# First attention of a two-block model: keys padded with zero rows, two value heads to a matmul

## The chip, the cores and the metric

The kernel runs on one core of one Trainium2 chip, as one program. The metric is the device time of one execution in microseconds (us). Engines are called as the profile calls them: PE is TensorE (PEld its weight loads), DVE is VectorE, ACT is ScalarE, POOL is GpSimd, SP is SyncE.

## The reference, cut

The whole reference is two blocks of two layers each, from window attention through latent attention and retention to a recurrent layer. The change lies in the first layer, the window attention: 16 query heads of 64, four key and value heads (each serves four query heads), 1024 tokens in 8 tiles of 128 rows, and 256 context rows in two more tiles. A token sees the context and the keys at most 128 positions away.

```python
def window_gqa(hx, hc, w_in, sink, w_out, cos, sin, need_ctx):
    q, k, v, g = jnp.split(h @ w_in, [A_WIDTH, A_WIDTH + A_KV_WIDTH, A_WIDTH + 2 * A_KV_WIDTH], axis=-1)
    qx = apply_rope(qx, cos, sin)
    kx = apply_rope(kx, cos, sin)
    ...
        s_loc = jnp.einsum("bqhgd,bkhd->bhgqk", q, k).astype(F32) * scale
        s_loc = jnp.where(m, s_loc, -jnp.inf)
        s_ctx = jnp.einsum("bqhgd,bchd->bhgqc", q, kc).astype(F32) * scale
        p = softmax_with_sink(jnp.concatenate([s_loc, s_ctx], axis=-1), sink_b).astype(v.dtype)
        return (jnp.einsum("bhgqk,bkhd->bqhgd", p[..., :3 * BLOCK], v)
                + jnp.einsum("bhgqc,bchd->bqhgd", p[..., 3 * BLOCK:], vc))
    ...
    sc = jnp.einsum("bqhgd,bkhd->bhgqk", qc, kc).astype(F32) * scale
    pc = softmax_with_sink(sc, sink_b).astype(vc.dtype)
    oc = jnp.einsum("bhgqk,bkhd->bqhgd", pc, vc).reshape(b, hc.shape[1], A_WIDTH)
```

## The kernel before

The program is a chain of stages. Each stage is a block with one stream of instructions for each engine, tied by semaphores, and ends in a barrier of all engines. The order within a stream is the order of the Python loops; there is no scheduler. All data is float32. P is 128, BANK (a PSUM bank) 512 columns, and PSUM has eight banks.

**Projections (`window_qkv`).** For each of the ten tiles (two of context, eight of tokens) PE multiplies the normed and transposed rows by the query weights (two products of 512 columns) and by the key and value weights `w_kv` (one of 512, L585 loads them). DVE applies the rotation to queries and keys. PE turns them (`turn_heads`), and ACT copies the result from PSUM into `qT` and `kT` (L615, L617). A pair of heads stands in one 128-partition column block of `qT`: 64 partitions for each. `kT` has two such blocks, for four key heads. Pair p of query heads uses block p // 4, its lower head the lower 64 partitions and its upper head the upper ones.

**Attention (`window_attend`).** The work is cut into U = 80 units, unit u being tile u // 8 and pair u % 8. `key_tiles` gives the key tiles of a unit: two for the 16 context units, four for the 16 units of tiles 2 and 9, five for the 48 others. In a step u of PE's loop stand `scores(u)`, `transposes(u - 1)`, `sixth_bank(u)` and `values(u - 2)`:
- `scores` multiplies queries by keys for both heads of the pair, each with 64 rows (its half of the partitions), a run of neighbouring key tiles at a time (L886), into two banks for each head.
- DVE (`maxima`, L831 or L828 for the context tiles) reads the scores, adds the mask, stores them in `s_sb` and finds the row's maximum; L834 makes the bias. `scores(u + 1)` waits for both of these reads.
- ACT (`exps`, L789) takes the exponentials. PE transposes them (`transposes`, L896, four key tiles a head; the fifth in `sixth_bank`, L906), and ACT (L782) and DVE (L841) copy them to `pT`.
- `values` multiplies the value head's 64 columns by `pT`, key tile by key tile, for each head apart (L923). The lower head's result goes to PSUM partitions 0 to 63, the upper one's to 64 to 127 of one bank, `o_bank`, which holds four units.
- After four units ACT copies `o_bank` to `oT` (L804); the next `values` waits for that (L919). `sixth_bank` also turns `oT` back (L910), seven steps late, and DVE multiplies by the reciprocal of the sums (L847).

SP issues one load in this stage, of weights for the next one, into the buffer `first_weights` (called `room` in `program`).

Of the kernel before, what the change touches and what calls it, by code (L numbers as in the profile page):

```python
# [9 lines left out]
F32 = mybir.dt.float32  # L10
# [3 lines left out]
P = 128  # L14
D = 1024
KD = D // P
# [542 lines left out]

def window_qkv(nc, core, a, qT, kT, v, w_q, q_in, x_in, hT, hT_dram, mask, mask_in, sink_rows, sink_in):  # L560

# [3 lines left out]
    with ExitStack() as mem:  # L565
        sb = lambda n, shape: mem.enter_context(nc.sbuf_tensor(f"{name}_{n}", shape, F32))
        w_kv, table = sb("w_kv", [P, KD, 2 * KV]), sb("table", [P, NT, 2, A_DIM])
        xn, squares, stat = sb("xn", [P, D]), sb("squares", [P, D]), sb("stat", [P, 2])
# [5 lines left out]
             "rope_k", "q_turned", "k_turned", "qT_moved", "kT_moved"))  # L574
        hT_stored = [nc.alloc_semaphore(f"{name}_hT_stored{k}") for k in range(2)]
        cond = lambda i: 1 if i < CTX_TILES else 0
        xT_banks, q_bank, kv_bank = core.banks(0, 2), [core.banks(2), core.banks(3)], core.banks(4)
        qT_banks, kT_bank = core.banks(5, 2), core.banks(7)[:, 0:2 * P]
        HALF_STEPS, K_STEPS = 4, 4
        with nc.Block() as block:  # L580
# [17 lines left out]
            def _(act):  # L598
# [14 lines left out]
                def turned(i):  # L613
                    act.wait_ge(q_turned, i + 1)
                    act.activation(qT[:, :, i * P:(i + 1) * P], qT_banks.rearrange("p (n t) -> p n t", n=WINDOW_PAIRS), ACT.Copy).then_inc(qT_moved, 1)  # L615
                    act.wait_ge(k_turned, i + 1)
                    act.activation(kT[:, :, i * P:(i + 1) * P], kT_bank.rearrange("p (g t) -> p g t", g=2), ACT.Copy).then_inc(kT_moved, 1)  # L617

                norm(1)
                for i in range(NT):  # L620
# [5 lines left out]
                    act.activation(v[:, i, :], kv_bank[:, KV:2 * KV], ACT.Copy).then_inc(v_moved, 1)  # L626
                turned(NT - 1)

            @block.vector
# [64 lines left out]
            def _(pe):  # L694
# [8 lines left out]
                def turn_heads(i):  # L703
                    pe.wait_ge(rope_q, (i + 1) * 2 * HALF_STEPS)
                    pe.wait_ge(qT_moved, i)
                    for n in range(WINDOW_PAIRS):
                        last = pe.transpose(qT_banks[:, n * P:(n + 1) * P], qr[:, n // 4, n % 4, :, :].rearrange("p b d -> p (b d)"), core.ident)
                    last.then_inc(q_turned, 1)
                    pe.wait_ge(rope_k, (i + 1) * K_STEPS)
                    pe.wait_ge(kT_moved, i)  # L710
                    for g in range(2):
                        last = pe.transpose(kT_bank[:, g * P:(g + 1) * P], kr[:, 2 * g:2 * g + 2, :].rearrange("p b d -> p (b d)"), core.ident)
                    last.then_inc(k_turned, 1)
# [20 lines left out]
def window_attend(nc, core, a, qT, kT, v, o, mask, mask_in, sink_rows, sink_in, prefetch):  # L734
# [11 lines left out]
    with ExitStack() as mem:  # L746
# [9 lines left out]
             "pv_made", "oT_moved", "over_steps", "over_made", "back_read"))  # L756
        s_banks = [core.banks(0, 2), core.banks(2, 2)]
        pT_banks, fifth_bank, o_bank = [core.banks(4), core.banks(5)], core.banks(6), core.banks(7)
        slot = lambda u, b: pair(u) * 2 + b
# [6 lines left out]
        with nc.Block() as block:  # L766
# [6 lines left out]
            def _(act):  # L773
# [18 lines left out]
                for u in range(U + BACK):  # L792
# [5 lines left out]
                    if u >= 5 and j == 0 and w < U // 4:  # L798
                        act.wait_ge(over_steps, 3 * w + 1)
                        act.activation(halves(over, w), halves(over, w), ACT.Exp).then_inc(over_made, 1)  # L800
                        act.wait_ge(pv_made, 4 * w + 4)
                        if w >= 2:
                            act.wait_ge(fifth_made, turned_by(4 * (w - 2) + 3 + BACK))
                        act.activation(oT[:, w % 2, :, :], o_bank.rearrange("p (j q) -> p j q", j=4), ACT.Copy).then_inc(oT_moved, 1)  # L804

            @block.vector
            def _(dve):
# [9 lines left out]
                def maxima(u):  # L817
# [7 lines left out]
                    for b in range(2):  # L825
                        k = slot(u, b)
                        if t < CTX_TILES:
                            dve.tensor_scalar(s_sb[:, u % 2, b, 0:n], s_banks[b][:, 0:n], 1.0, NEG, ALU.mult, ALU.max,  # L828
                                              accum_out=smax[:, par, k:k + 1]).then_inc(s_read, 1)
                        else:  # L830
                            dve.tensor_tensor_reduce(out=s_sb[:, u % 2, b, 0:n], in0=s_banks[b][:, 0:n], in1=mask[:, lo:lo + n], scale=1.0,  # L831
                                                     scalar=NEG, op0=ALU.add, op1=ALU.max, accum_out=smax[:, par, k:k + 1]).then_inc(s_read, 1)
# [38 lines left out]
            def _(pe):  # L871
                def scores(u):
                    t, p = tile(u), pair(u)
                    if u:
                        pe.wait_ge(s_read, 2 * u)
                    runs, at = [], 0
                    for k in tiles(u):
                        if runs and runs[-1][0] + runs[-1][1] == k and at % BANK:
                            runs[-1][1] += 1
                        else:  # L880
                            runs.append([k, 1, at])
                        at += P
                    for k, n, at in runs:
                        for b in range(2):
                            rows = slice(b * A_DIM, (b + 1) * A_DIM)
                            last = pe.matmul(s_banks[b][:, at:at + n * P], qT[rows, p, t * P:(t + 1) * P], kT[rows, p // 4, k * P:(k + n) * P],  # L886
                                             start=True, stop=True)
                    last.then_inc(s_made, 1)
# [10 lines left out]
                def sixth_bank(u):  # L899
# [7 lines left out]
                    if u >= BACK:  # L907
                        n = u - BACK
                        pe.wait_ge(oT_moved, n // 4 + 1)
                        last = pe.transpose(fifth_bank[:, 2 * P:3 * P], oT[:, (n // 4) % 2, n % 4, :], core.ident)  # L910
                    last.then_inc(fifth_made, 1)

                def values(u):
# [4 lines left out]
                    if u >= 4 and u % 4 == 0:  # L918
                        pe.wait_ge(oT_moved, u // 4)  # L919
                    for n, k in enumerate(tiles(u)):  # L920
                        for b in range(2):
                            rows, g = slice(b * A_DIM, (b + 1) * A_DIM), (p // 4) * 2 + b
                            last = pe.matmul(o_bank[rows, (p % 4) * P:(p % 4 + 1) * P], v[:, k, g * A_DIM:(g + 1) * A_DIM], pT[:, u % 2, b, n, :],  # L923
                                             start=(n == 0), stop=(n == len(tiles(u)) - 1))
                    last.then_inc(pv_made, 1)
# [3434 lines left out]
def program(nc, a, out):  # L4360
    with ExitStack() as mem:
# [12 lines left out]
        with ExitStack() as layer:  # L4374
# [7 lines left out]
            with ExitStack() as keys:  # L4382
                qT = keys.enter_context(nc.sbuf_tensor("window_qT", [P, WINDOW_PAIRS, ALL_TILES * P], F32))
                kT = keys.enter_context(nc.sbuf_tensor("window_kT", [P, 2, ALL_TILES * P], F32))
                v = keys.enter_context(nc.sbuf_tensor("window_v", [P, ALL_TILES, A_KV * A_DIM], F32))
# [3 lines left out]
                with stage(nc):  # L4389
                    window_qkv(nc, core, a, qT, kT, v, o[:, 0:KD, :], q_in, x_in, hT, window_hT, mask, mask_in, sink_rows, sink_in)  # L4390
                with stage(nc):
# [116 lines left out]
```

## Time and profile before

| | us |
|---|---|
| median of 3 runs | 4081.69 |
| lowest, highest | 4074.6, 4082.69 |
| span of the profiled execution, first to last instruction | 4072.7 |
| projections stage, about | 36 to 265 of the span |
| attention stage, about | 266 to 543 of the span |

The page gives the profiled execution by its span alone. The span is the yardstick for everything read from the trace; the three runs give the times. In a timeline, a row is a run of like instructions of one engine: its start, the time from its first start to its last end, the engine, the line, the operation, the tiles and the count. A float32 matmul leaves two records on PE (a transpose leaves one), and two loads. Ends of matmuls are modelled and overlap the next one's start, so steps are read from start to start.

### The profile page before, as it was taken

Reading aid. Unit: us, or ns where it says so; the run is one execution under the profiler, and the core shown is the slowest. Engines: PE = TensorE matmul, PEld = TensorE weight load, DVE = VectorE, ACT = ScalarE, POOL = GpSimd, SP = SyncE. Lnnn points to the kernel's source line nnn. Section 1 sums busy time; section 2 is a strip of 40 time slices with the busy share of each in tenths; the row PEclk is TensorE's granted clock in tenths of the full one; section 3 lists DMA queues with packets and bytes.
Section 4 is the critical chain, followed back from the end, with each engine's and each line's share of the span. In section 5 each row is a group of like instructions: output and inputs, shape, how many; then the busy total and the mean of one; then the engine's idle time right before and its main releaser. Section 6 shows DMA issues by size and latency. Waiting matters only on the chain. (4 is left out here: it accounts for less than half of the span.)

```text
span 4072.7 us, 70205 instructions
## 1 busy us (share of the span) xinstructions
PE 3849.9 (95%) x29666; PEld 2300.5 (56%) x29666; DVE 1705.5 (42%) x3625; ACT 1216.5 (30%) x2209; POOL 803.2 (20%) x491
## 2 busy tenths in 40 slices
PE   8999999989999999999998998997999988988998
PEld 3458854445456666644554446443544468888643
DVE  3346643232144444432332008225644466565422
ACT  1147731112256556411221009112200132222124
POOL 0000023400000000142000000333112126675442
PEclk9999999999999999999999999998999999999999
DMA  6000033242321010212002000111232221212301
GB/s 227 21 21 2 2 104 114 83 103 84 118 81 39 24 48 25 74 42 73 32 16 104 16 16 28 62 42 27 83 132 85 80 86 61 70 45 88 114 6 41
DMA packets 174413, 256.15 MB, mean 63 GB/s; under 512 B 50596, under 2 KB 96148, under 8 KB 174102
## 3 DMA queue, kind: packets, MB, share of 16 engines
q1 hardware_dynamic: 174104, 251.67, 17.9%
q8 instruction: 238, 3.90, 0.4%
q14 instruction: 71, 0.58, 0.0%
HBM read 189.33 MB, written 62.05 MB: 62 GB/s over the span
## 5 line engine op out<-in xcount | busy, mean ns | idle before, releaser
L2185 DVE TENSOR_SCALAR_CACHE_REDUCE la_s<-psum 128x512 f32<-128x512 f32 (+1 forms) x384 | 210.3, 598 | 192.0 <-PE psum L2251 191.8
L2158 ACT ACTIVATE la_pT<-psum 128x512 f32<-128x512 f32 x320 | 173.0, 594 | 216.8 <-PE psum L2261 216.8
L963 POOL TENSOR_TENSOR lg_seven_s<-other_columns 128x512 f32<-128x512 f32 x4 | 5.1, 1265 | 891.4 <-POOLq L112 870.9
L2149 ACT ACTIVATE la_s<-la_s,la_negm 128x1280 f32<-128x1280 f32 x128 | 174.6, 1364 | 18.6 <-DVE la_negm L2194 14.8
L270 PE MATMUL psum<-room,columns 128*128 128x512 f32 x400 | 173.4, 592 | 0.4 <-DMA room<-in_even_w_in_dram 0.4
L2261 PE MATMUL psum<-ident,la_s 128*128 128x128 f32 x1280 | 166.2, 277 | 0.1
L2261 PEld LDWEIGHTS psum<-ident,la_s 128*128 128x128 f32 x1280 | 138.9, 140 | 40.7 <-issue 35.2
L4266 PE MATMUL psum<-rs_inverse,rs_Z 64*64 64x64 f32 x2560 | 156.3, 223 | 5.7 <-DVE rs_Z L4118 2.8
L4264 PE MATMUL psum<-rs_Z,rs_inverse 64*64 64x64 f32 x2048 | 135.6, 224 | 17.3 <-DVE rs_Z L4118 16.5
L2245 PE MATMUL psum<-la_kT,la_qT 64*128 64x512 f32 (+1 forms) x672 | 143.0, 544 | 7.4 <-DVE la_s L2185 7.4
L4266 PEld LDWEIGHTS psum<-rs_inverse,rs_Z 64*64 64x64 f32 x2560 | 136.7, 139 | 7.5 <-issue 7.3
L963 POOL TENSOR_TENSOR pg_seven_s<-pg_other_pair 128x512 f32<-128x512 f32 x4 | 6.5, 1623 | 675.6 <-ACT pg_other_pair L2863 675.6
L2272 PE MATMUL psum<-la_pT,la_v 128*64 128x128 f32 x2240 | 134.6, 275 | 0.7 <-ACT la_pT L2158 0.7
L831 DVE CUSTOM_DVE_ANT_0 wa_s<-psum,window_mask_rows 128x640 f32<-128x640 f32 (+1 forms) x128 | 100.7, 787 | 71.5 <-PE psum L886 71.5
L270 PEld LDWEIGHTS psum<-room,columns 128*128 128x128 f32 x400 | 75.9, 190 | 96.4 <-issue 96.1
L4264 PEld LDWEIGHTS psum<-rs_Z,rs_inverse 64*64 64x64 f32 x2048 | 117.9, 140 | 20.2 <-issue 18.6
L2272 PEld LDWEIGHTS psum<-la_pT,la_v 128*64 128x64 f32 x2240 | 121.2, 137 | 10.1 <-issue 9.0
L963 POOL TENSOR_TENSOR wg_seven_s<-other_columns 128x512 f32<-128x512 f32 x5 | 6.3, 1269 | 591.6 <-POOLq L112 543.8
L4126 DVE TENSOR_TENSOR rs_inverse<-rs_inverse,psum 128x512 f32<-128x512 f32 (+1 forms) x160 | 101.1, 632 | 45.2 <-PE psum L4266 44.5
L789 ACT ACTIVATE wa_s<-wa_s,wa_negm 128x640 f32<-128x640 f32 (+2 forms) x160 | 117.3, 742 | 0.4 <-DVE wa_negm L834 0.3
L4251 PE MATMUL psum<-rs_inverse,rs_A 64*64 64x64 f32 x2560 | 107.2, 222 | 10.5 <-DVE rs_inverse L4112 8.8
L984 PE MATMUL psum<-rp_t,rp_seven_s 128*128 128x512 f32 x256 | 115.7, 595 | 0.0
(674 smaller groups left out, 8198.8 us busy)
## 6 DMA issues: line engine op xcount, KB each, us to landing
later_slot<-in_ada_w_dram SPq DMA_DIRECT2D x16, 1024.0 KB
rwkv_raw<-x_rows SPq DMA_DIRECT2D x64, 256.0 KB, 2.0
room<-rwkv_raw SPq DMA_DIRECT2D x32, 512.0 KB, 4.7
room<-in_even_w_in_dram SPq DMA_DIRECT2D x6, 2048.0 KB, 9.4
room<-in_odd_w_in_dram SPq DMA_DIRECT2D x6, 2048.0 KB, 12.7
ada_slots<-in_ada_w_dram SPq DMA_DIRECT2D x8, 1024.0 KB, 9.4
rwkv_raw<-room SPq DMA_DIRECT2D x16, 512.0 KB, 2.6
latent_v<-lp_v SPq DMA_DIRECT2D x10, 512.0 KB, 2.8
```

The lines of the kernel that those rows point to most:

```text
L270: last = pe.matmul(out[:, c:c + w], left[:, k, :], right[:, k, c:c + w], start=(k == 0), stop=(k == kd - 1))
L789: act.activation(s_sb[:, u % 2, b, 0:n], s_sb[:, u % 2, b, 0:n], ACT.Exp, scale=SCALE, bias=negm[:, par, k:k + 1], accum_out=total[:, par, ...
L984: last = pe.matmul(bank, left[:, k, :], right[:, k, :], start=fresh and k == 0, stop=k == HK - 1, skip_group_check=True)
L2149: act.activation(s_sb[:, g % 2, j, :], s_sb[:, g % 2, j, :], ACT.Exp, bias=negm[:, g % 2, j:j + 1], accum_out=total[:, g % 2, j:j + 1]).th ...
L2158: act.activation(pT[:, h, at * BANK:(at + 1) * BANK], pT_banks[turn], ACT.Copy).then_inc(pT_moved[turn], 1)
L2185: dve.tensor_scalar(s_sb[:, g % 2, j, cols], s_banks[j][:, 0:cols.stop - cols.start], SCALE, NEG, ALU.mult, ALU.max, accum_out=smax[:, g % ...
L2245: pe.matmul(s_banks[unit(h, i)][:, 0:width], q_of[rows, queries(i)], k_of[rows, cols], start=True, stop=False)
L2261: last = pe.transpose(pT_banks[turn][:, n * P:(n + 1) * P], s_sb[:, g % 2, j, t * P:(t + 1) * P], core.ident)
L2272: last = pe.matmul(o_banks[h][i * B_V:(i + 1) * B_V, 0:P], v_of[:, t, h * B_V:(h + 1) * B_V], pT[:, h, i * K + t * P:i * K + (t + 1) * P], ...
L4251: last = pe.matmul(core.banks(2 + m % 2)[chunk(c), n * C:(n + 1) * C], A[chunk(c), 0, h, 0, :], T[chunk(c), h, :], start=True, stop=True)
L4264: pe.matmul(bank[chunk(c), n * C:(n + 1) * C], TT[chunk(c), h, :], Z[chunk(c), h, :], start=True, stop=True)
L4266: last = pe.matmul(bank[chunk(c), (GH + n) * C:(GH + n + 1) * C], Z[chunk(c), h, :], TT[chunk(c), h, :], start=True, stop=True)
```

## The change

Keys. `kT` gets four blocks in place of two, one for each key head: its 64 rows stand where its query head's rows stand in `qT`, and the other 64 partitions are zero. POOL writes the zeros (four memsets) during the projections. ACT copies the keys in two instructions of 64 partitions where it had one of 128. The room for the wider `kT` comes from `w_kv`, which moves to the buffer `first_weights`.

Scores. Each head's scores are one product over all 128 partitions with both heads' queries; the rows of the other head meet zeros. The scores of both heads stand one behind the other in three banks instead of two and two, cut where a bank ends.

Values. One matmul for each key tile covers both heads: stationary are two value heads' 128 columns, moving are both heads' 256 columns of `pT`. The result is 128x256, of which two of four quarters are wanted. Four units need two banks (`o_banks`), and ACT copies the wanted quarters in two instructions.

```diff
-        w_kv, table = sb("w_kv", [P, KD, 2 * KV]), sb("table", [P, NT, 2, A_DIM])
+        table = sb("table", [P, NT, 2, A_DIM])
...
-                    act.activation(kT[:, :, i * P:(i + 1) * P], kT_bank.rearrange("p (g t) -> p g t", g=2), ACT.Copy).then_inc(kT_moved, 1)
+                    for b in range(2):
+                        rows = slice(b * A_DIM, (b + 1) * A_DIM)
+                        act.activation(kT[rows, b:A_KV:2, i * P:(i + 1) * P], kT_bank[rows, :].rearrange("p (g t) -> p g t", g=2), ACT.Copy).then_inc(kT_moved, 1)
...
+            @block.gpsimd
+            def _(pool):
+                for b in range(2):
+                    other = slice((1 - b) * A_DIM, (2 - b) * A_DIM)
+                    for g in range(2):
+                        pool.memset(kT[other, 2 * g + b, :], 0.0).then_inc(padded, 1)
+                pool.wait_ge(padded, A_KV)
...
-        s_banks = [core.banks(0, 2), core.banks(2, 2)]
-        pT_banks, fifth_bank, o_bank = [core.banks(4), core.banks(5)], core.banks(6), core.banks(7)
+        s_banks, o_banks = core.banks(0, 3), core.banks(3, 2)
+        pT_banks, fifth_bank = [core.banks(5), core.banks(6)], core.banks(7)
+        scores_of = lambda u, b: s_banks[:, b * len(tiles(u)) * P:(b + 1) * len(tiles(u)) * P]
+        o_of = lambda j: o_banks[:, j * 2 * P:(j + 1) * 2 * P]
...
-                        act.activation(oT[:, w % 2, :, :], o_bank.rearrange("p (j q) -> p j q", j=4), ACT.Copy).then_inc(oT_moved, 1)
+                        for b in range(2):
+                            rows = slice(b * A_DIM, (b + 1) * A_DIM)
+                            act.activation(oT[rows, w % 2, :, :], o_banks[rows, :].rearrange("p (j b q) -> p j b q", j=4, b=2)[:, :, b, :], ACT.Copy).then_inc(oT_moved, 1)
...
-                    runs, at = [], 0
-                    for k in tiles(u):
...
-                    for k, n, at in runs:
-                        for b in range(2):
-                            rows = slice(b * A_DIM, (b + 1) * A_DIM)
-                            last = pe.matmul(s_banks[b][:, at:at + n * P], qT[rows, p, t * P:(t + 1) * P], kT[rows, p // 4, k * P:(k + n) * P],
-                                             start=True, stop=True)
+                    for b in range(2):
+                        runs, at = [], b * len(tiles(u)) * P
+                        for k in tiles(u):
...
+                        for k, n, at in runs:
+                            last = pe.matmul(s_banks[:, at:at + n * P], qT[:, p, t * P:(t + 1) * P], kT[:, 2 * (p // 4) + b, k * P:(k + n) * P], start=True, stop=True)
...
-                        for b in range(2):
-                            rows, g = slice(b * A_DIM, (b + 1) * A_DIM), (p // 4) * 2 + b
-                            last = pe.matmul(o_bank[rows, (p % 4) * P:(p % 4 + 1) * P], v[:, k, g * A_DIM:(g + 1) * A_DIM], pT[:, u % 2, b, n, :],
-                                             start=(n == 0), stop=(n == len(tiles(u)) - 1))
+                        last = pe.matmul(o_of(p % 4), v[:, k, (p // 4) * 2 * A_DIM:(p // 4 + 1) * 2 * A_DIM], pT[:, u % 2, :, n, :],
+                                         start=(n == 0), stop=(n == len(tiles(u)) - 1))
...
-                kT = keys.enter_context(nc.sbuf_tensor("window_kT", [P, 2, ALL_TILES * P], F32))
+                kT = keys.enter_context(nc.sbuf_tensor("window_kT", [P, A_KV, ALL_TILES * P], F32))
...
-                    window_qkv(nc, core, a, qT, kT, v, o[:, 0:KD, :], q_in, x_in, hT, window_hT, mask, mask_in, sink_rows, sink_in)
+                    window_qkv(nc, core, a, qT, kT, v, o[:, 0:KD, :], room, q_in, x_in, hT, window_hT, mask, mask_in, sink_rows, sink_in)
```

PE's stream in a unit of five key tiles, before (matmuls are listed once each; the last number is the shape written, partitions by columns):

```order
L886 MATMUL psum<-window_kT,window_qT 128x256 x4
L886 MATMUL psum<-window_kT,window_qT 128x128 x2
L896 MATMUL psum<-ident,wa_s 128x128 x8
L906 MATMUL psum<-ident,wa_s 128x128 x2
L910 MATMUL psum<-ident,wa_oT 128x128
L923 MATMUL psum<-wa_pT,window_v 64x128 x10
```

The same unit after:

```order
L900 MATMUL psum<-window_kT,window_qT 128x256 x2
L900 MATMUL psum<-window_kT,window_qT 128x128
L900 MATMUL psum<-window_kT,window_qT 128x256
L900 MATMUL psum<-window_kT,window_qT 128x128 x3
L909 MATMUL psum<-ident,wa_s 128x128 x8
L919 MATMUL psum<-ident,wa_s 128x128 x2
L923 MATMUL psum<-ident,wa_oT 128x128
L934 MATMUL psum<-wa_pT,window_v 128x256 x5
```

Six score matmuls become seven, ten values matmuls of 64x128 become five of 128x256; the order of the four groups and the eleven transposes stay. The second place is ACT's stream around the copy to `oT` in the units of four and five key tiles, before:

```order
L789 ACTIVATE wa_s,wa_total<-wa_s,wa_negm 128x512 x2
L800 ACTIVATE wa_over<-wa_over 128x8
L804 ACTIVATE wa_oT<-psum 128x512
L782 ACTIVATE wa_pT<-psum 128x512 x2
L789 ACTIVATE wa_s,wa_total<-wa_s,wa_negm 128x512 x2
```

and after:

```order
L802 ACTIVATE wa_s,wa_total<-wa_s,wa_negm 128x512 x2
L813 ACTIVATE wa_over<-wa_over 128x8
L819 ACTIVATE wa_oT<-psum 64x512 x2
L795 ACTIVATE wa_pT<-psum 128x512 x2
L802 ACTIVATE wa_s,wa_total<-wa_s,wa_negm 128x512 x2
```

One copy becomes two of half the partitions, at the same place.

## Rows read from the trace of the kernel before

**Rows 1.** The page's head: the span, and PE's busy time and instructions.

```profile
span 4072.7 us, 70205 instructions
...
PE 3849.9 (95%) x29666; PEld 2300.5 (56%) x29666; DVE 1705.5 (42%) x3625; ACT 1216.5 (30%) x2209; POOL 803.2 (20%) x491
```

**Rows 2.** Busy time by stretch: start:end, length, busy us (count) of each engine.

```profile
core 0: us, PE busy (x) PEld busy (x) DVE busy (x) ACT busy (x) POOL busy (x), PEclk, DMA share, GB/s
60.00:265.00 205.00, 203.37 (x596) 98.86 (x594) 73.33 (x135) 27.51 (x58) 0.00 (x0) 1.00 0.04 17
...
361.00:392.00 31.00, 31.00 (x348) 26.61 (x346) 21.10 (x71) 22.74 (x53) 0.00 (x0) 1.00 0.01 1
```

**Rows 3.** Waits of 300 to 530 us: total us, times, the longest.

```profile
DVE wa_s L831 <- PE psum L886: 69.8, 62, 1.4
ACT wa_pT L782 <- PE psum L896: 57.9, 61, 1.2
...
PE psum L886 <- DVE wa_smax L831: 0.4, 1, 0.4
```

**Rows 4.** Timeline of PE, one unit of five key tiles: start, us, line, count.

```profile
400.02 1.35 PE L886 MATMUL psum<-window_kT,window_qT 64*128 64x256 f32 x12
401.31 1.09 PE L896 MATMUL psum<-ident,wa_s 128*128 128x128 f32 x8
402.24 0.38 PE L906 MATMUL psum<-ident,wa_s 128*128 128x128 f32 x2
402.46 0.27 PE L910 MATMUL psum<-ident,wa_oT 128*128 128x128 f32 x1
402.66 1.31 PE L923 MATMUL psum<-wa_pT,window_v 128*64 128x128 f32 x20
403.90 0.49 PE L886 MATMUL psum<-window_kT,window_qT 64*128 64x256 f32 x2
```

**Rows 5.** Timeline of PE, a unit of four key tiles (tile 9).

```profile
518.92 1.14 PE L886 MATMUL psum<-window_kT,window_qT 64*128 64x256 f32 x8
519.99 1.09 PE L896 MATMUL psum<-ident,wa_s 128*128 128x128 f32 x8
...
521.12 1.09 PE L923 MATMUL psum<-wa_pT,window_v 128*64 128x128 f32 x16
522.14 1.14 PE L886 MATMUL psum<-window_kT,window_qT 64*128 64x256 f32 x8
```

**Rows 6.** Timeline of PE, a unit of two key tiles: its scores and the next unit's.

```profile
288.29 0.70 PE L886 MATMUL psum<-window_kT,window_qT 64*128 64x256 f32 x4
...
290.20 0.70 PE L886 MATMUL psum<-window_kT,window_qT 64*128 64x256 f32 x4
```

**Rows 7.** Timeline of PE, dense runs on the full array in other stages.

```profile
232.24 1.04 PE L707 MATMUL psum<-ident,wq_qr 128*128 128x128 f32 x8
...
233.33 7.03 PE L270 MATMUL psum<-wq_w_kv,columns 128*128 128x512 f32 x16
...
2535.62 1.95 PE L2744 MATMUL psum<-stick_v,sk_wT 128*128 128x128 f32 x16
```

**Rows 8.** Groups by line and shape, 264 to 545 us: busy us, mean ns, idle before.

```profile
L886 PEld LDWEIGHTS psum<-window_kT,window_qT 64*128 64x128 f32 x800 | 69.5, 187 | 22.5 <-issue 12.7 <-DVE wa_s L828 3.8 <-DVE wa_smax L831 1.0
...
L804 ACT ACTIVATE wa_oT<-psum 128x512 f32<-128x512 f32 x20 | 11.8, 590 | 1.7 <-PE psum L923 1.7
...
L963 POOL TENSOR_TENSOR wg_seven_s<-other_columns 128x512 f32<-128x512 f32 x1 | 1.3, 1264 | 543.8 <-POOLq L112 543.8
```

**Rows 9.** Timeline: the last keys of the projections, the last copy of the attention.

```profile
263.94 0.44 PE L712 MATMUL psum<-ident,wq_kr 128*128 128x128 f32 x2 [1.02 <-DVE wq_kr L679]
264.42 0.38 ACT L617 ACTIVATE window_kT<-psum 128x256 f32<-128x256 f32 x1 [0.43 <-PE psum L712]
...
539.22 0.60 ACT L804 ACTIVATE wa_oT<-psum 128x512 f32<-128x512 f32 x1 [1.73 <-PE psum L923]
```

**Rows 10.** One line of another stage, its weight loads: ns min/median/max.

```profile
L2744 PEld LDWEIGHTS psum<-stick_v,sk_wT x288: 186/192/333, 2445.1 to 2548.0; 128*128 128x128 f32 x144
```

More of the change, by code:

```diff
@@ L557, with window_qkv @@
 WINDOW_PAIRS = A_HEADS // 2
-def window_qkv(nc, core, a, qT, kT, v, w_q, q_in, x_in, hT, hT_dram, mask, mask_in, sink_rows, sink_in):
+def window_qkv(nc, core, a, qT, kT, v, w_q, w_kv, q_in, x_in, hT, hT_dram, mask, mask_in, sink_rows, sink_in):
     name = "wq"
@@ L575, in window_qkv @@
         hT_stored = [nc.alloc_semaphore(f"{name}_hT_stored{k}") for k in range(2)]
+        padded = nc.alloc_semaphore(f"{name}_padded")
         cond = lambda i: 1 if i < CTX_TILES else 0
@@ L709, in turn_heads @@
                     pe.wait_ge(rope_k, (i + 1) * K_STEPS)
-                    pe.wait_ge(kT_moved, i)
+                    pe.wait_ge(kT_moved, 2 * i)
                     for g in range(2):
@@ L827, in maxima @@
                         if t < CTX_TILES:
-                            dve.tensor_scalar(s_sb[:, u % 2, b, 0:n], s_banks[b][:, 0:n], 1.0, NEG, ALU.mult, ALU.max,
+                            dve.tensor_scalar(s_sb[:, u % 2, b, 0:n], scores_of(u, b), 1.0, NEG, ALU.mult, ALU.max,
                                               accum_out=smax[:, par, k:k + 1]).then_inc(s_read, 1)
                         else:
-                            dve.tensor_tensor_reduce(out=s_sb[:, u % 2, b, 0:n], in0=s_banks[b][:, 0:n], in1=mask[:, lo:lo + n], scale=1.0,
+                            dve.tensor_tensor_reduce(out=s_sb[:, u % 2, b, 0:n], in0=scores_of(u, b), in1=mask[:, lo:lo + n], scale=1.0,
                                                      scalar=NEG, op0=ALU.add, op1=ALU.max, accum_out=smax[:, par, k:k + 1]).then_inc(s_read, 1)
@@ L875, in scores @@
                         pe.wait_ge(s_read, 2 * u)
-                    runs, at = [], 0
-                    for k in tiles(u):
[L878 to L882, printed above, removed]
-                    for k, n, at in runs:
-                        for b in range(2):
-                            rows = slice(b * A_DIM, (b + 1) * A_DIM)
-                            last = pe.matmul(s_banks[b][:, at:at + n * P], qT[rows, p, t * P:(t + 1) * P], kT[rows, p // 4, k * P:(k + n) * P],
-                                             start=True, stop=True)
+                    for b in range(2):
+                        runs, at = [], b * len(tiles(u)) * P
+                        for k in tiles(u):
+                            if runs and runs[-1][0] + runs[-1][1] == k and at % BANK:
+                                runs[-1][1] += 1
+                            else:
+                                runs.append([k, 1, at])
+                            at += P
+                        for k, n, at in runs:
+                            last = pe.matmul(s_banks[:, at:at + n * P], qT[:, p, t * P:(t + 1) * P], kT[:, 2 * (p // 4) + b, k * P:(k + n) * P], start=True, stop=True)
                     last.then_inc(s_made, 1)
@@ L908, in sixth_bank @@
                         n = u - BACK
-                        pe.wait_ge(oT_moved, n // 4 + 1)
+                        pe.wait_ge(oT_moved, 2 * (n // 4 + 1))
                         last = pe.transpose(fifth_bank[:, 2 * P:3 * P], oT[:, (n // 4) % 2, n % 4, :], core.ident)
@@ L918, in values @@
                     if u >= 4 and u % 4 == 0:
-                        pe.wait_ge(oT_moved, u // 4)
+                        pe.wait_ge(oT_moved, 2 * (u // 4))
                     for n, k in enumerate(tiles(u)):
-                        for b in range(2):
-                            rows, g = slice(b * A_DIM, (b + 1) * A_DIM), (p // 4) * 2 + b
-                            last = pe.matmul(o_bank[rows, (p % 4) * P:(p % 4 + 1) * P], v[:, k, g * A_DIM:(g + 1) * A_DIM], pT[:, u % 2, b, n, :],
-                                             start=(n == 0), stop=(n == len(tiles(u)) - 1))
+                        last = pe.matmul(o_of(p % 4), v[:, k, (p // 4) * 2 * A_DIM:(p // 4 + 1) * 2 * A_DIM], pT[:, u % 2, :, n, :],
+                                         start=(n == 0), stop=(n == len(tiles(u)) - 1))
                     last.then_inc(pv_made, 1)
```

## The prediction

> **What bounds the kernel now.** I read the page's head first: PE is busy 95% of a span of 4072.7 us [rows 1]. The change touches two stages, so next the busy times by stretch [rows 2]: the projections (60 to 265 us) keep PE busy 203.4 of 205 us, with DVE at 73 and ACT at 28; in the attention, 361 to 392 us, PE is busy 31.00 of 31.00 us, ACT 22.7 and DVE 21.1, at a granted clock of 1.00, the upper level, 2.4 GHz. The waits of 300 to 530 us say who waits for whom [rows 3]: DVE waited 69.8 us for the scores and ACT 57.9 us for the transposes, while PE waited once, for 0.4 us. So here each ns added to PE's queue is a ns of the stage, and a ns added to ACT or DVE is free as long as it fits under PE.
>
> The stage is 80 units (ten query tiles by eight head pairs). In its steady part a unit takes 3.88 us, from 400.02 to 403.90 [rows 4]: scores 1.29, eleven transposes 1.35, values 1.24. With four key tiles a unit takes 3.22 us (518.92 to 522.14) [rows 5], with two 1.91 [rows 6]. There are 48 units of five key tiles, 16 of four, 16 of two.
>
> **How PE's time is made.** Each float32 matmul leaves two records (six score matmuls, x12). The full-array price comes from dense runs elsewhere [rows 7]. Sixteen records of 512 columns span 7.03 us; less the last one's own 0.592 that is 15 steps of 0.429. Sixteen of 128 columns span 1.95; less 0.275 it is 15 steps of 0.112. A straight line through both gives 0.218 for 256 columns. Transposes go at (1.04 - 0.273) / 7 = 0.110.
>
> Now the same sizes when two records use different halves of the array. The values matmuls of before write 64 columns each, one head in either half: 16 records of 128 columns span 1.09 us [rows 5], where the full array needs 1.95 for the same 16 records [rows 7]. Scores have 64 rows each and do the same: 8 records of 256 columns are followed by the next line after 1.07 us [rows 5], where the full array would need 8 x 0.218 = 1.74. **The halves run side by side**; a record of half the array streams as long as one of the whole array, but two go at once. The change gives this up on both products. The padding rows are zeros, yet they are multiplied; in the values product half of the 128x256 result (one head's weights by the other's values) is thrown away.
>
> The Trainium skill says this as a rule ("TensorE: Matmul & The Clock Gate", Why this matters for your kernels): a matmul with few rows takes the time of a full one, and the gain lies in tiles that run at the same time. It speaks against this change, and the rows above agree (1.09 against 1.95 us).
>
> **Part 1: scores.** After, a unit of five key tiles has seven matmuls, as the second head's stretch begins at column 640 and is cut at the bank's edge: three of 256 and four of 128 columns, so 6 x 0.218 + 8 x 0.112 = 2.20 us, against 1.29.
>
> **Part 2: values.** Five matmuls of 256 columns: 10 x 0.218 = 2.18 us, against 1.24.
>
> **Part 3: the switches of array shape go.** Before, a unit passes from 64-row to full to 64-column matmuls and back. At the steady prices its paired work would be 4 x 0.218 + 2 x 0.112 = 1.10 (scores), 10 x 0.112 = 1.12 (values) and 11 x 0.110 = 1.21 (transposes), 3.43 in all; it takes 3.88 [rows 4]. The 0.45 us left are three joints of 0.15, each where the line and the shape change; between the transposes of L896, L906 and L910, where the line and the waited semaphore change but not the shape, 402.24 - 401.31 is 0.93 for eight and 0.22 for two, close to the steady 0.88 and 0.22. I therefore put the 0.45 down to the shape and let it go: transposes 1.35 becomes 1.21. The other end is that all 0.45 stays, since these joints are also where PE's loads wait for another engine's semaphore.
>
> The Trainium skill has this too ("TensorEngine Tiling (Array Packing)", Key Properties): changing the tiling mode drains TensorE. It names no price; by it the joints go entirely, which is the end taken. It would speak for the change, but 0.45 us is a quarter of what parts 1 and 2 add.
>
> **Sum for PE.** Five tiles: 2.20 + 1.21 + 2.18 = 5.59, so +1.71 a unit, x 48 = +82.1 us. Four tiles: tile 2 has scores 4 x 0.218 + 8 x 0.112 = 1.77, tile 9 has 8 x 0.218 = 1.74; nine transposes 0.99; values 8 x 0.218 = 1.74; 4.49 against 3.22, +1.27 x 16 = +20.3. Two tiles: 0.87 + 0.55 + 0.87 = 2.29 against 1.91 [rows 6], and the loop of DVE's maxima, which waits for the whole pair of scores, lengthens by at most the scores' own 0.44; I take +0.40 x 16 = +6.4.
>
> **Part 4: ACT, DVE, POOL and SP.** The copy of the output columns is split by partition halves; each half still has 512 elements a partition, so it costs 0.59 again [rows 8], 0.15 us a unit. The 31 us of 361 to 392 hold eight five-tile units: ACT's 22.7 make 2.84 a unit, with the second copy 3.0, under 5.59; DVE's 21.1 make 2.6, and it does the same operations after [rows 2]. Score banks are three in place of four, still with one unit in them: the next scores wait for both reads, as before. All of DVE's work of a unit is 2.6 us, and PE spends 1.21 + 2.18 = 3.39 us between a unit's scores and the next: covered. Before ACT has copied the output banks, the next group's values must wait (L919 and its counterpart); PE has the next unit's scores and transposes, 3.4 us, in between, against two copies, 1.2. Only at the end nothing covers the second copy: 539.22 begins the last one, and PE's last four transposes wait for it [rows 9]: +0.6. In the projections the key copy costs 0.38 more per tile on an ACT that is 13% busy; the last one stands on the way to the barrier [rows 9]: +0.4. Four memsets of 64x1280 on POOL: no row shows them; POOL's nearest row is 1.26 us for 512 columns of two inputs [rows 8], so 3.2 each and 12.6 in all, in a stage of 230 us in which POOL does nothing and nobody waits for it but the barrier. Cost 0; at the far end DVE slows meanwhile by 12.6 us, but PE waited for DVE there for 1.0 us at the last tile [rows 9], and POOL is done long before: at most 1 us comes through. The key and value weights go into an idle buffer by the same DMA in the same place of SP's queue: 0.
>
> Total: 82.1 + 20.3 + 6.4 + 0.6 + 0.4 = **+109.8 us**. Later stages have the same instructions and start that much later. The page gives the profiled execution's span, 4072.7 us, so its span after should be about 4182.5; the median of the three runs is 9.0 above the span (4081.7), and I add the same 9.0: **4191.5 us**, 2.7% slower.
>
> **Rivals.** (a) The joints keep their 0.45 us, for semaphores and not shape cause them: 64 long units x 0.45 and 16 short ones x 0.3 add 34 us, 4225. For it: each joint has a waiting load. Against: the transposes' own joints are free.
> (b) Faster: PE is paced by the number of records, not by columns. A five-tile unit falls from 43 records to 14 + 11 + 10 = 35; at 3.88 / 43 = 0.090 a record it would take 3.16 us, and 64 units would save some 45 us, 4037. It decides if a record of 256 columns costs less than two paired records do. Against it: 0.429 for 512 and 0.112 for 128 columns [rows 7]. I see nothing for it but the loads: the stage's 800 score loads take 187 ns each [rows 8].
> (c) No change to speak of: PE's added time is hidden. It would need another engine as the bound; DVE and ACT idle 8 to 10 of 31 us [rows 2]. 4082.
> (d) Loads of the full array don't hide under matmuls. A five-tile unit has 24 records with loads of 0.19 us [rows 10], +4.6 us in line, and the stage would grow by some 290 us beyond the forecast, 4480. The row against it: 16 records with such loads stand 0.112 apart [rows 7].
> The Trainium skill states (d) in the same page on TensorE (Part 3: Packing small matmuls): loads overlap running matmuls only when the row group differs. The trace does not agree for dense full-array runs.
>
> **How the numbers follow.** Forecast 0.82; (a) 0.11; (b) 0.03; (c) 0.02; (d) 0.02. Low end: all prices at their smallest (0.215 for 256 columns, 0.110 for 128) take 0.08 us from each long unit, -5, and the run-to-run spread of before (4074.6 to 4082.7) takes 8 more: with 5 for covers I misjudge, 4173. High end: (a) at 4225 and a little spread, 4228. A measurement can tell 0.2%, 8 us, from no change. Faster 0.03, same 0.02, slower 0.95.
>
> **What would show it.** The score line: 14 records in a five-tile unit, about 2.2 us; the values line: 10 records, about 2.2 us; no pairs that start together; unit period 5.6 us; stage 265 to about 652 us; DVE's and ACT's waits for PE grow by some 100 us each; joints of 0.11 us. If the period is near 6.0 the joints stayed (a); under 3.9 is (b). I am wrong altogether if a 256-column full-array record takes much less than 0.21 us there.

## The result and the profile after

The changed kernel takes 4191.26 us (median of 4 runs, 4182.68 to 4199.24), the kernel before, in four runs on the same chips, 4080.98. The ratio is 1.0275, with a 95% interval from 1.0263 to 1.0287: slower, by 110 us. The forecast was 4191.5.

The head of the page after answers to [rows 1], and the stretches of one query tile (eight units of five key tiles and a fraction) to [rows 2]:

```profile
span 4192.3 us, 69088 instructions
...
PE 3963.9 (95%) x29090; PEld 2432.1 (58%) x29090; DVE 1706.6 (41%) x3625; ACT 1234.6 (29%) x2239; POOL 808.5 (19%) x495
...
430.00:475.00 45.00, 45.00 (x285) 41.66 (x284) 21.11 (x70) 24.40 (x56) 0.00 (x0) 1.00 0.00 1
```

PE is busy 114 us longer with 576 matmul records fewer. In the units of five key tiles it is never idle, before and after. One unit of five key tiles, PE's timeline, answers to [rows 4]:

```profile
441.39 2.35 PE L900 MATMUL psum<-window_kT,window_qT 128*128 128x256 f32 x14
443.58 1.04 PE L909 MATMUL psum<-ident,wa_s 128*128 128x128 f32 x8
444.45 0.38 PE L919 MATMUL psum<-ident,wa_s 128*128 128x128 f32 x2
444.67 0.27 PE L923 MATMUL psum<-ident,wa_oT 128*128 128x128 f32 x1
444.78 2.33 PE L934 MATMUL psum<-wa_pT,window_v 128*128 128x256 f32 x10
446.94 0.38 PE L900 MATMUL psum<-window_kT,window_qT 128*128 128x256 f32 x1
```

From start to start: scores 2.19 us (before 1.29), transposes 1.20 (1.35), values 2.16 (1.24), the unit 5.55 (3.88). The waits of 300 to 640 us answer to [rows 3]; of the two engines that feed on PE, DVE waits 98 us longer and ACT 87:

```profile
DVE wa_s L846 <- PE psum L900: 168.2, 63, 3.0
ACT wa_pT L795 <- PE psum L909: 144.4, 65, 2.9
```

The next stage's first instruction started at 544.12 us before and starts at 654.50 now, so the two touched stages hold 110.4 us.

### The profile page after: what moved, and what is told of

Same layout as the page of the kernel before. It is cut to its first block and busy times, and to the rows that moved or that the text cites. A ratio compares the mean times of both kernels' runs of the same rounds, so it can differ in the third digit from the quotient of the medians.

```text
span 4192.3 us, 69088 instructions
## 1 busy us (share of the span) xinstructions
PE 3963.9 (95%) x29090; PEld 2432.1 (58%) x29090; DVE 1706.6 (41%) x3625; ACT 1234.6 (29%) x2239; POOL 808.5 (19%) x495
## 5 line engine op out<-in xcount | busy, mean ns | idle before, releaser
L900 PE MATMUL psum<-window_kT,window_qT 128*128 128x256 f32 (+1 forms) x896 | 163.2, 332 | 3.7 <-PEq L112 2.0
L934 PE MATMUL psum<-wa_pT,window_v 128*128 128x256 f32 x672 | 158.6, 380 | 1.5 <-ACT wa_oT L819 1.5
L900 PEld LDWEIGHTS psum<-window_kT,window_qT 128*128 128x128 f32 x896 | 144.5, 193 | 21.0 <-DVE wa_s L843 3.4
L270 PE MATMUL psum<-first_weights,columns 128*128 128x512 f32 x288 | 133.9, 620 | 15.1 <-PEq L112 15.1
L934 PEld LDWEIGHTS psum<-wa_pT,window_v 128*128 128x128 f32 x672 | 121.8, 191 | 15.3 <-issue 2.1
## 6 DMA issues: line engine op xcount, KB each, us to landing
room<-in_odd_w_in_dram SPq DMA_DIRECT2D x6, 2048.0 KB, 12.6
```

The costliest lines, as they stand in the source:

```text
L270: last = pe.matmul(out[:, c:c + w], left[:, k, :], right[:, k, c:c + w], start=(k == 0), stop=(k == kd - 1))
L900: last = pe.matmul(s_banks[:, at:at + n * P], qT[:, p, t * P:(t + 1) * P], kT[:, 2 * (p // 4) + b, k * P:(k + n) * P], start=True, stop=True)
L934: last = pe.matmul(o_of(p % 4), v[:, k, (p // 4) * 2 * A_DIM:(p // 4 + 1) * 2 * A_DIM], pT[:, u % 2, :, n, :], start=(n == 0), stop=(n == ...
```

## The experiments

Each kernel differs in the attention stage alone, unless said. "Unit" is the distance from one unit's scores to the next one's in PE's timeline, with five key tiles.

**1. The scores alone.** The changed kernel, with the values of before and one copy of the output bank.

```diff
-                        last = pe.matmul(o_of(p % 4), v[:, k, (p // 4) * 2 * A_DIM:(p // 4 + 1) * 2 * A_DIM], pT[:, u % 2, :, n, :],
+                        for b in range(2):
+                            rows, g = slice(b * A_DIM, (b + 1) * A_DIM), (p // 4) * 2 + b
+                            last = pe.matmul(o_bank[rows, (p % 4) * P:(p % 4 + 1) * P], v[:, k, g * A_DIM:(g + 1) * A_DIM], pT[:, u % 2, b, n, :],
```

> The scores as in the changed kernel (padded keys, whole array, one bank run for both heads), the values as before (two heads side by side, one copy to oT). Theory (columns decide, halves run side by side, and a joint of 0.15 us stands where the array's shape changes): the joint between scores and transposes goes, the two around the values stay. A unit of five key tiles: 2.19 + 1.21 + 0.15 + 1.12 + 0.15 = 4.82 us against 3.88; 48 x 0.94 + 16 x 0.71 + 16 x 0.25 = +61 us, ratio 1.015. If the joints come from semaphores, all three stay: 4.97 us, +73 us, 1.018. If records decide and not columns: 45 records against 43, about 4.06 us, +12 us.

Measured: ratio 1.0161 (1.0144 to 1.0178), 4141.3 us. PE's timeline of a unit:

```profile
441.73 2.45 PE L897 MATMUL psum<-window_kT,window_qT 128*128 128x256 f32 x14
444.02 1.04 PE L906 MATMUL psum<-ident,wa_s 128*128 128x128 f32 x8
444.89 0.38 PE L916 MATMUL psum<-ident,wa_s 128*128 128x128 f32 x2
445.11 0.27 PE L920 MATMUL psum<-ident,wa_oT 128*128 128x128 f32 x1
445.31 0.88 PE L933 MATMUL psum<-wa_pT,window_v 128*64 128x128 f32 x12
```

The unit is 4.83 us, against 4.82 (joints by shape), 4.97 (joints by semaphores) and 4.06 (records). A joint is the time lost where PE passes from one group of matmuls to the next. From L920 to L933, where the shape changes, is 0.20 us; in the changed kernel, from L923 to L934 at the same place and with the same waits, it is 0.11.

**2. The values alone.** The kernel before, with one matmul of 256 columns for each key tile. Two banks for the output don't fit beside four for the scores, so the bank holds two units.

```diff
-                            last = pe.matmul(o_bank[rows, (p % 4) * P:(p % 4 + 1) * P], v[:, k, g * A_DIM:(g + 1) * A_DIM], pT[:, u % 2, b, n, :],
+                        last = pe.matmul(o_bank[:, (p % 2) * 2 * P:(p % 2 + 1) * 2 * P], v[:, k, (p // 4) * 2 * A_DIM:(p // 4 + 1) * 2 * A_DIM], pT[:, u % 2, :, n, :],
```

> The values as in the changed kernel (one matmul of 256 columns a key tile), the scores and the keys as before (two heads side by side in four banks). As banks are short, the output bank holds two units and is copied every two units in two half copies. Theory: a unit of five key tiles takes 1.09 + 0.15 + 1.21 + 2.16 + 0.15 = 4.76 us against 3.88; 48 x 0.88 + 16 x 0.67 + 16 x 0.25 = +57 us, ratio 1.014, with a few us more where the twice as frequent copies are not covered (units of two key tiles). Joints from semaphores: 4.91 us, +69 us. Records decide: 33 records, 2.97 us, -60 us.

Measured: ratio 1.0153 (1.0137 to 1.0169), 4139.9 us; the unit is 4.80 us, against 4.76 (joints by shape), 4.91 (joints by semaphores) and 2.97 (records). Either half of the change alone costs about as much as the other. Together their units add 0.95 + 0.92 = 1.87 us, where both at once add 1.67: the third joint, from values to scores, goes only when both are on the whole array. That explains 0.15 of the 0.20. The other 0.05 is what the two units lie above their sums (0.04 here, 0.01 in experiment 1); where it comes from is not shown.

**3. The same matmuls, not side by side.** The kernel before, with the loops over heads and over key tiles exchanged, in scores and values.

```diff
-                    for n, k in enumerate(tiles(u)):
-                        for b in range(2):
+                    for b in range(2):
+                        for n, k in enumerate(tiles(u)):
```

> The kernel before with the same matmuls of half the array, but in another order: first all of the lower head, then all of the upper one, in the scores and in the values, so that neighbours use the same half. Theory (the gain of before lies in running side by side): the scores of five key tiles cost 8 x 0.216 + 4 x 0.112 = 2.18 us and the values 20 x 0.112 = 2.24, the joints stay; a unit takes 2.18 + 1.21 + 2.24 + 0.45 = 6.08 us, in all about +144 us, ratio 1.035. Rival (a matmul on half the array is cheaper by itself, whatever stands beside it): 3.88 us as before, 1.000.

Measured: ratio 1.0175 (1.0160 to 1.0190), 4147.2 us.

```profile
452.68 2.02 PE L923 MATMUL psum<-wa_pT,window_v 128*64 128x128 f32 x20
454.63 1.89 PE L886 MATMUL psum<-window_kT,window_qT 64*128 64x256 f32 x12
456.45 1.09 PE L896 MATMUL psum<-ident,wa_s 128*128 128x128 f32 x8
```

The same 20 records of half the array take 1.95 us in this order and 1.24 in the order of before, the same 12 score records 1.82 and 1.29. So a matmul on half the array is not cheap by itself; its neighbour makes it cheap. But the unit is 5.12 us, not 6.08: the theory was right in kind and wrong in size. In the trace the upper head's first values record starts (453.39 us) when the lower head's seventh of ten does (453.38), so the lower head's last four run side by side with the upper's first four, and the 20 records take 16 steps of 0.11. In the scores the upper head starts with the lower one's third of six (455.17 and 455.16 us). And with two key tiles (four values records a head) the unit takes 1.92 us in either order. From this a new theory: PE issues in order, and either half can hold four records, the running one among them. By it the upper head's first record goes in as soon as the lower's last is held, four from the end: the seventh of ten, the third of six.

**4. A fourth change of shape.** The kernel before, with the fifth tiles' and the output's transposes behind the values.

```diff
+                    if 2 <= u <= U + 1:
+                        values(u - 2)
                     if turns[u]:
                         sixth_bank(u)
-                    if 2 <= u <= U + 1:
-                        values(u - 2)
```

> The kernel before with the fifth tiles' and the output's transposes (one to three of the whole array) moved behind the values of the same step. The same matmuls and the same waits on semaphores; the shape of the array now changes four times a unit and not three times. Joints from the shape: +0.15 us a unit, 4.03 us for five key tiles, 80 x 0.15 = +12 us, ratio 1.003. Joints from semaphores: 3.88 us, 1.000.

Measured: ratio 1.0030 (1.0019 to 1.0042), 4090.4 us, some 12 us more than before.

```profile
442.40 1.35 PE L886 MATMUL psum<-window_kT,window_qT 64*128 64x256 f32 x12
443.68 1.09 PE L896 MATMUL psum<-ident,wa_s 128*128 128x128 f32 x8
444.70 1.31 PE L923 MATMUL psum<-wa_pT,window_v 128*64 128x128 f32 x20
445.95 0.44 PE L906 MATMUL psum<-ident,wa_s 128*128 128x128 f32 x2
446.22 0.27 PE L910 MATMUL psum<-ident,wa_oT 128*128 128x128 f32 x1
446.42 0.49 PE L886 MATMUL psum<-window_kT,window_qT 64*128 64x256 f32 x2
```

The unit is 4.03 us, 0.15 more than before with the same matmuls and the same waits. Units of two and of four key tiles lengthen by the same 0.15 (1.92 to 2.07, 3.22 to 3.37). The joints come from the shape of the array. The Trainium skill's rule ("TensorEngine Tiling (Array Packing)", Key Properties) is that a change of the tiling mode drains TensorE. The trace agrees as far as it goes: a change costs 0.15 us.

**5 and 6. How far apart the neighbours may be.** The kernel before, with the values in groups of two key tiles a head, and of three (the diff is that of three).

```diff
-                    for n, k in enumerate(tiles(u)):
-                        for b in range(2):
+                    order = [(n, k, b) for lo in range(0, len(tiles(u)), 3) for b in range(2) for n, k in list(enumerate(tiles(u)))[lo:lo + 3]]
+                    for n, k, b in order:
```

> The kernel before with the values in another order: two key tiles of the lower head (four records), two of the upper, and so on, instead of head by head within a key tile. The unpaired order, tested before, showed that the upper head's first record starts while three records of the lower head are still to come. Theory (PE issues in order, and each half of the array can hold four records, the running one among them): groups of four records lose nothing, a unit of five key tiles stays at 3.88 us. Rival (the two halves work together only for neighbours in program order): only every group's edge pairs; the values need 10 - 5 = some 15 steps of 0.11 in place of 10, unit about 4.4 us.

> The same with groups of three key tiles (six records a head, then four). Theory of four records a half: the upper head starts two steps late, 12 steps in place of 10, a unit of five key tiles takes 3.88 + 0.22 = 4.10 us, one of four 3.22 + 0.22 = 3.44. If any depth were held: 3.88.

One run of each; values and next scores in PE's timeline, groups of two first:

```profile
444.81 1.36 PE L924 MATMUL psum<-wa_pT,window_v 128*64 128x128 f32 x20
446.10 1.13 PE L886 MATMUL psum<-window_kT,window_qT 64*128 64x256 f32 x8
```

```profile
442.06 1.58 PE L924 MATMUL psum<-wa_pT,window_v 128*64 128x128 f32 x20
443.57 1.35 PE L886 MATMUL psum<-window_kT,window_qT 64*128 64x256 f32 x12
```

The values take 1.29 us and 1.51 us, against 1.24 in pairs; the units are 3.93 and 4.15. The step from two to three is the 0.22 us of the theory; both are 0.05 above it. The rival of neighbours only (some 4.4 us) is out. A depth of four records fits experiments 3, 5 and 6. By three the upper head of experiment 3 would have started with the lower's eighth record, by five with its sixth; it started with the seventh.

**7. Columns or records, on the whole array.** The changed kernel with the 256 columns in two halves.

```diff
-                        last = pe.matmul(o_of(p % 4), v[:, k, (p // 4) * 2 * A_DIM:(p // 4 + 1) * 2 * A_DIM], pT[:, u % 2, :, n, :],
+                            last = pe.matmul(o_of(p % 4)[:, b * P:(b + 1) * P], v[:, k, (p // 4) * 2 * A_DIM:(p // 4 + 1) * 2 * A_DIM], pT[:, u % 2, b, n, :],
```

> The changed kernel with each values matmul of 256 moving columns cut into two of 128, one for each head, still on the whole array (head after head). Columns decide: 20 x 0.112 = 2.24 us in place of 10 x 0.216 = 2.16, a unit of five key tiles 5.63 us against 5.55. Records decide: the values' time doubles, some 7.7 us.

One run: twice the records, unit 5.62 us against 5.55. Columns decide.

```profile
443.78 2.40 PE L935 MATMUL psum<-wa_pT,window_v 128*128 128x128 f32 x20
446.01 1.25 PE L900 MATMUL psum<-window_kT,window_qT 128*128 128x256 f32 x6
```

**8. The second copy.** In the changed kernel every fourth unit of two key tiles takes 2.97 us (the first of them 3.08) and the others 2.28. Before, it was 2.14 to 2.20, and 1.91 to 1.94. The rows of PE, then of ACT, there:

```profile
293.44 1.02 PE L900 MATMUL psum<-window_kT,window_qT 128*128 128x256 f32 x4
295.48 1.10 PE L934 MATMUL psum<-wa_pT,window_v 128*128 128x256 f32 x4 [0.46 <-ACT wa_oT L819]
...
294.14 1.19 ACT L819 ACTIVATE wa_oT<-psum 64x512 f32<-64x512 f32 x2
```

PE has 1.4 us of other work after 293.44, scores and transposes. ACT begins the copies 0.7 us after that point, behind its exponentials, and they take 1.2.

The copy of the upper half was moved to DVE, at the same step:

```diff
+                        dve.tensor_copy(oT[A_DIM:P, w % 2, :, :], o_banks[A_DIM:P, :].rearrange("p (j b q) -> p j b q", j=4, b=2)[:, :, 1, :]).then_inc(oT_moved, 1)
```

> The changed kernel with the second half copy of the output banks on DVE, beside ACT's. Theory: in the units of two key tiles every fourth step of 2.97 us, in which PE waits for the second copy, falls towards 2.5 us, 4 x 0.5 = 2 us in all, and the end of the stage comes some 0.6 us sooner; the units of four and five key tiles stay at 4.46 and 5.55 us. If these steps are long for another reason, they stay at 2.97.

One run: these steps are 2.36 us (the first 2.47), 0.61 less, and the long units stay as they were (4.47 and 5.55). So the long step was the second copy. There are three such steps among the short units, not the four of the expectation: 1.8 us in all. The other half of the expectation failed: the end of the stage comes 0.63 us later, not 0.6 sooner. From the start of the last copy to the next stage's first instruction it is 5.89 us (644.17 to 650.06) against 5.26 (649.24 to 654.50). DVE's last sums and reciprocals stand behind its copy and now come after it (644.89 and 645.10), so PE's next transpose starts 1.56 us after the copies began and not 1.35. The other 0.4 us lie in the transposes that follow, at a granted clock of 0.70 (644.1 to 650) where it was 1.00. The single time, 4176.6 us, is 14.6 below the changed kernel's median, but a single run cannot measure a gain of 1 us: the changed kernel's own runs differ by 17.

**9. Use the halves more, not less.** The experiments say that transposes too should gain from halves. A transpose multiplies by the identity, and two of the identity's quarters are zero. So each transpose of the kernel before is cut into two, each of 64 rows of the scores and the 64 identity columns that belong to them, for either half of the array, with the results in different banks; ACT copies both heads after one wait. The fifth tiles' and the output's transposes stay whole, for want of a bank.

```diff
-                            last = pe.transpose(pT_banks[b][:, n * P:(n + 1) * P], s_sb[:, u % 2, b, n * P:(n + 1) * P], core.ident)
-                        last.then_inc(pT_made, 1)
+                            for h in range(2):
+                                half = slice(h * 64, (h + 1) * 64)
+                                at = b * 4 * 64 + n * 64
+                                last = pe.transpose(pT_banks[h][:, at:at + 64], s_sb[half, u % 2, b, n * P:(n + 1) * P], core.ident[half, half])
+                    last.then_inc(pT_made, 1)
```

> The kernel before, with the first four transposes a head cut into two of 64 rows and 64 columns each, one for either half of the array (the other quarters of the identity are zero and are left out), the halves written to different banks; ACT copies both heads at once. Nothing is left out of the result. Theory (halves side by side, columns decide): a pair of halves streams 64 columns and takes 0.055 us in place of 0.109, eight pairs save 0.44 us, and the joint between scores and transposes moves to the one ahead of the fifth tiles; a unit of five key tiles takes 3.44 us, in all up to -32 us, ratio 0.992. Rival (a record has a least time, or its weight load has, near 0.05 us each): the pair takes as long as one whole transpose, 3.88 us, 1.000; and if ACT's joint copy is late, more than that.

Measured: ratio 0.9961 (0.9947 to 0.9974), 4058.3 us against 4078.2: 20 us less. That is under half a per cent, but the interval leaves out 1. It beats both kernels.

```profile
440.06 1.35 PE L887 MATMUL psum<-window_kT,window_qT 64*128 64x256 f32 x12
441.25 0.66 PE L900 MATMUL psum<-ident,wa_s 64*128 64x64 f32 x16
441.84 0.44 PE L910 MATMUL psum<-ident,wa_s 128*128 128x128 f32 x2
442.11 0.27 PE L914 MATMUL psum<-ident,wa_oT 128*128 128x128 f32 x1
442.32 1.31 PE L927 MATMUL psum<-wa_pT,window_v 128*64 128x128 f32 x20
443.56 1.35 PE L887 MATMUL psum<-window_kT,window_qT 64*128 64x256 f32 x12
```

The unit is 3.50 us. Sixteen halves take 0.59 us, where eight whole ones took 0.93 [rows 4]. From scores to transposes it is 1.19 us and no longer 1.29, as the shape stays. The 0.59 holds the change of shape behind it: the first pair starts at 441.25 us, the eighth at 441.68 and the next line at 441.84. So a pair costs 0.061 us, not the 0.055 of its columns, and the change 0.10 at this place. Eight pairs save 8 x (0.109 - 0.061) = 0.38 us, which is the whole gain of the unit (3.88 to 3.50); what sets the 0.061 stays open. The units of two key tiles get longer, 2.07 us on average against 1.98. Those of four (3.22 before) take 3.0 to 3.1 and not the 2.78 that 0.44 less would give: there the loads of the second head's transposes begin only when ACT's exponentials end (506.12 and 506.07 us in one unit). So 20 us come where 32 was the upper estimate.

## Why the prediction was right, point by point

- **PE is the bound, and each ns of its queue counts.** Right: PE is busy 45.00 of 45.00 us, and the unit grew by what PE's rows grew. DVE's and ACT's waits for PE grew by 98 and 87 us (forecast some 100 each).
- **The price of the whole array.** Right. The scores took 2.19 us (forecast 2.20), the values 2.16 (2.18). The straight line gave 0.218 for 256 columns and the values' record takes 2.16 / 10 = 0.216: 0.04 us a unit.
- **The halves run side by side.** Right, and shown by experiment 3 on the same matmuls. What the trace of before could not show is that they need not be neighbours: a record of the upper half starts while three of the lower half are still to come.
- **The joints go with the shape.** Right: transposes 1.20 (1.21), and experiment 4 prices a joint at 0.15 us by itself. Rival (a) is out.
- **Long units.** 48 x 1.67 = 80.2 us (forecast 82.1); those of four key tiles 4.47 and 4.44 us (4.49), about +19.7 (20.3).
- **Short units.** The term was too small: from the first unit's scores to the seventeenth's, 16 units, 32.17 us (265.94 to 298.11) became 41.81 (266.68 to 308.49), +9.6 (forecast 6.4). The step that failed is the cover of the second copy, which I worked out for the long units and took as good for all. In a short one PE has 0.87 + 0.55 = 1.4 us of other work, and the second copy came late three times (0.60, 0.46 and 0.46 us); experiment 8 puts it at 1.8 us in all. Another 2.3 us lie in the first three units, 10.15 us against 7.87 in experiment 8. There 270 to 275 us had a granted clock of 0.50, the lower level of 1.2 GHz, after; it was 0.82 before and 0.90 in experiment 8. What is left, 5.5 us, is experiment 8 against the kernel before, and is below the 6.4. That the change lowers the clock there is not shown: over 265 to 300 us it was 0.85 after and 0.95 before, but also 0.95 in experiments 7 and 8, which have its scores, and 0.85 in experiment 9, a form of the kernel before. The stretches of the two kernels, before and then after:

```profile
270.00:275.00 5.00, 5.00 (x36) 2.85 (x36) 2.40 (x12) 4.21 (x16) 0.00 (x0) 0.82 0.62 240
...
270.00:275.00 5.00, 4.74 (x12) 3.42 (x13) 1.37 (x7) 2.54 (x10) 0.00 (x0) 0.50 0.76 295
```

- **The two ends.** Right in the sum: the last copy takes 1.21 us, not 0.60 [rows 9], and the last key copies 0.78, not 0.38. From the start of the last copy to the next stage only 0.36 us were added (4.90 to 5.26), as PE's granted clock there was 1.00 after and 0.73 before; and the projections' last key transposes came 0.34 us later (263.94 and 264.28 us), which was not followed.

```profile
264.76 0.78 ACT L620 ACTIVATE window_kT<-psum 64x256 f32<-64x256 f32 x2 [0.42 <-PE psum L723]
...
649.24 1.21 ACT L819 ACTIVATE wa_oT<-psum 64x512 f32<-64x512 f32 x2 [2.98 <-PE psum L934]
```

- **The memsets.** Free, as forecast. They are also cheaper than the 12.6 us taken from a row of two inputs: 5.12 us for all four, done at 41.4 us, before anything there is late.

```profile
36.32 5.12 POOL L637 MEMSET window_kT<- 64x1280 f32 x4 [35.87 <-POOLq L112]
```

- **From span to time.** This step was wrong, and the error is hidden. I took the 9.0 us between the span and the median as time around the span. The profiled execution after has a time of 4194.06 us and a span of 4192.3, so 1.8 us lie around it. The 9.0 were the scatter of executions: before, the profiled one was most likely the fastest of the three (4074.6 is 1.9 above its span). As median was compared with median, the sum is not hurt. But the spans differ by 119.6 us, 9.2 more than the two stages hold. It is the recurrent scan of the last layer, which the change does not touch: 528 us before and 538 after, with the same 13548 matmuls and a lower clock. PE's busy time holds 4.3 of the 10 us; where the rest comes from is not shown. Before, then after:

```profile
3301.00:3829.00 528.00, 469.83 (x13548) 440.14 (x13549) 332.40 (x530) 114.31 (x177) 326.54 (x146) 0.97 0.21 71
```

```profile
3411.00:3949.00 538.00, 474.10 (x13548) 444.61 (x13549) 333.97 (x530) 115.37 (x178) 327.25 (x146) 0.96 0.20 70
```

- **The total.** The medians differ by 110.3 us (forecast 109.8), the two stages by 110.4. That the total fits to half a us is luck: the short units lie 3.2 above their term and the long ones 2.5 below, and runs of one kernel differ by more than either.

The rivals (b), (c) and (d) are out: records don't pace PE (experiments 2 and 7), nothing hid PE's time, and the loads of 0.19 us lay under the matmuls: fourteen score records in 2.19 us, where their loads alone would be 2.7. For (d) the Trainium skill's sentence ("TensorE: Matmul & The Clock Gate", Part 3: Packing small matmuls) that loads overlap only across row groups does not agree with this trace. The prediction took that sentence alone; the same part also lets a load into the background weight buffer be pulled ahead, and that would fit the trace.

## What to carry to other kernels

Where two products each fill half the array and stand near each other in PE's queue, they can already run together; filling the other half with zeros, or with columns that are thrown away, took 1.7 times as long here (1.29 to 2.19 us, 1.24 to 2.16). Count PE's time in columns streamed and in changes of shape, and look whether full-width work with zeros in it (a transpose by the identity) can be cut into halves instead. A cover that is worked out for the commonest unit has to be worked out again for the shortest.

## What the runs showed of the hardware

- A change of the array's shape (64 rows, whole, 64 columns) costs 0.15 us (experiment 4: 3.88 to 4.03 us a unit). The stage before has three of them in each of 80 units, by estimate some 36 us.
- The halves overlap over a distance, as if each held four records: groups of four records a half cost 0.05 us, groups of six 0.27, groups of ten 0.71 (1.24, 1.29, 1.51 and 1.95 us for the same 20 records).
- Transposes in float32 run on halves by rows: a pair of pieces (64 rows and 64 moving columns each) takes 0.061 us against 0.109 for a whole one (experiment 9).
- Executions of one kernel differ by up to 17 us (4182.7 to 4199.2), and of the difference between the two profiled spans 10 us lay in a stage where PE's granted clock was 0.96 instead of 0.97.
